# Norms by token tile, four memory slabs in the RWKV chain and two before the cross attention's queries

## The chip, the cores and the metric

One core of one Trainium2 chip runs the kernel. The metric is the device time of one execution in microseconds (us). Before the change it was 943.74 us, the median of three runs (943.54 to 943.77).

## The reference

256 tokens of width 1024 in float32 pass two blocks. Cut to what matters here:

```
h = rmsnorm(x, ln1);  z = h @ w_in            # q, k, v of three attentions, three gates
x = x + merged @ w_o
u = conv(rmsnorm(x, ln2) @ w_up);  x = x + (silu(a) * b) @ w_down
x = rmsnorm(x, ln_f)
mem_n = rms_norm(mem, mem_norm_g);  kv = mem_n @ wkv      # 1024 -> 2048
p = rms_norm(x, g[0]) @ w_in_first            # conformer conv and RWKV-7
y = concat([y_conv, y_rwkv]) @ w_out;   x = x + rms_norm(y, g[1])
q = rms_norm(x, g[2]) @ wq;  y = attention(q, kv) @ wo;   x = x + rms_norm(y, g[3])
y = swiglu(rms_norm(x, g[4]), w_gu) @ w_down; x = x + rms_norm(y, g[5])
```

rmsnorm(x, g) is x / sqrt(mean(x^2) + eps) * g along the 1024 features.

## The kernel before

**Numbers.** Every large product is made three times in fp32r: high part by high part, high by low, low by high (`three`, L1507 to L1509). An operand's high part is a ScalarE copy to fp32r (`w_hi`, `hT_hi`), its low part VectorE's difference (`w_lo`, `hT_lo`).

**Weights.** They come as 126 slabs of 1 MB in the order of their use. SyncE loads them into four buffers `raw`, ScalarE makes the high part (`split`, L457), VectorE the low part (L876), each into two buffers. TensorE waits for the low part of slab n (`lo_ready`) and signals `slab_used`, which frees the buffers for slab n+2. `splits(n)` in the programs of ScalarE and VectorE marks where in their own order slabs up to n are split.

**Products.** The tokens are two tiles (TT = 2) of 128, the features eight (KD = 8). `features` takes a slab of 256 output columns: 2 x 8 x 3 products, each with 128 columns of weights as the stationary side and all 256 tokens as the moving one. `token_products` makes results by token in the PSUM banks 4 to 7 (w_o, down, out2, wo2, down2). ScalarE and VectorE evacuate (L531 in qkv, L616 in up, L663 in in2, L804 in wq, L846 in gu2).

**A norm.** ScalarE: for each token tile a square with its sum (`sumsq`, L470) and the root (L476). VectorE: the reciprocal (L906) and x times it (`normed`, L913). When both tiles are there, TensorE transposes feature tiles 0 to 3 of both tokens into two banks and 4 to 7 after these were read (`transposes`, L1537). ScalarE copies the high part with the gain as a scale per partition (L489), VectorE makes the low part (L924). The order of all this is written out by hand in each engine's program, with semaphores between. In y1, y3 and y5 (`add_normed`) VectorE multiplies the PSUM result by reciprocal and gain row (L1420) and adds it to x (L1423).

**Memory.** The kv product of the cross attention needs only the memory tokens, so its eight slabs serve as filling: `MEM_A` = 2 after down, `MEM_B` = 5 in the RWKV chain, cut into groups of three products that `fill(point)` issues at the places listed in `MEM_FILL`, and `MEM_C` = 1 behind out2. The chain has four chunks c with the points r, u and s each, then y's sum, the products with "center" (L1996), the point gc, the head sums (L1778) and the spreads in out2's second slab.

**Queues.** GpSimd issues the small loads, the gain rows for ln_f, y1, y3 and y5 (`load_row_gain`) and the memory tokens, and multiplies the convolution's taps into diagonals (L433) after x of down is ready. ScalarE loads all masks in one DMA at the start. SyncE loads x, waits for it, loads slab 0, waits for the masks, loads the rest.

Of the kernel before, what the change touches and what calls it, by code (L numbers as in the profile page):

```python
# [17 lines left out]
F32 = mybir.dt.float32  # L18
# [31 lines left out]
MEM_A, MEM_B, MEM_C = 2, 5, 1  # L50
# [35 lines left out]
VEC_PARTS = (("ln1", 8), ("ln2", 8), ("g0", 8), ("g2", 8), ("g4", 8), ("mem_g", 8), ("mu", 14),  # L86
# [3 lines left out]
for _name, _count in VEC_PARTS:  # L90
# [6 lines left out]
TRANSPOSED = ("ln1", "ln2", "mem", "g0", "g2", "g4")  # L97
STATS = {"ln1": 0, "ln2": 1, "mem": 2, "ln_f": 3, "g0": 4, "y1": 5, "g2": 6, "y3": 7, "g4": 8, "y5": 9}
# [8 lines left out]
MASK_PARTS = (("ident", P), ("ones_head", P), ("ones_all", P), ("strict_st", CHUNK),  # L107
              ("incl_st", CHUNK), ("ident_st", CHUNK), ("scan", T), ("eps", 1), ("ln_eps", 1), ("gn_eps", 1),
# [6 lines left out]
MASK_COLS = _n  # L115
# [30 lines left out]
def mem_place(i):  # L146
# [11 lines left out]
    "consts_in", "masks_ready", "x_in", "small_in", "bias_rows_out", "bias_in", "row_gain_in", "mem_in", "y_out",  # L158
# [30 lines left out]
def transposed_bank(name, k):  # L189

    return k // 2 if name == "mem" else 2 + k // 2 % 2
# [21 lines left out]
def build(nc, x_in, mem_in, weights, fb_w, pairs_vec, vec_in, rows_in, masks_in, late_in, onehot_in, table_in,  # L213
          row_small, lora_in, bias_scratch, out):
    with ExitStack() as ctx:
# [24 lines left out]
        row_gain = sb("row_gain", [P, D])  # L240

# [41 lines left out]
        pvec = sb("pvec", [P, PAIRS, 16], F32, feed)  # L283
# [81 lines left out]
        def _(sp):  # L365
            for t in range(TT):
                sp.dma_start(x[:, t, :], x_in[0, t * P:(t + 1) * P, :]).then_inc(sems["x_in"], 16)
# [21 lines left out]
            sp.wait_ge(sems["y_out"], 16 * TT)  # L389
# [3 lines left out]
        def _(pool):  # L393
            pool.dma_start(vec[:, :], vec_in).then_inc(sems["consts_in"], 16)
# [9 lines left out]

            load_row_gain(0, 0)

# [16 lines left out]
            pool.wait_ge(sems["x_ready"], X_READY["w_o"] + TT)  # L423
# [16 lines left out]
            load_row_gain(1, 0)  # L440
            load_row_gain(2, X_READY["y1"] + TT)
            load_row_gain(3, X_READY["y3"] + TT)
# [3 lines left out]
        def _(act):  # L446
# [3 lines left out]
            act.dma_start(masks[:, 0:MASK_COLS], masks_in).then_inc(sems["masks_ready"], 16)  # L450
# [13 lines left out]
            def sumsq(name, src, waits=None):  # L464

                q = STATS[name]
                for t in range(TT):
                    if waits:
                        waits(t)
                    A(ub[:, 1, :, :, :].rearrange("p a b n -> p (a b n)") if name == "mem" else xn[:, t, :], src(t), ACT.Square,  # L470
                      accum_out=stat[:, 4 * q + t:4 * q + t + 1]).then_inc(sems["sumsq_ready"], 1)
# [11 lines left out]
            def fill_normed(name):  # L483

                z, col = TRANSPOSED.index(name), VEC["mem_g" if name == "mem" else name]
                dst = hTm_hi if name == "mem" else hT_hi
                for k in range(KD):
                    act.wait_ge(sems["xt_ready"], 4 * z + k // 2 + 1)
                    A(dst[:, k, :], ps[:, transposed_bank(name, k), k % 2 * T:k % 2 * T + T], ACT.Copy,  # L489
                      scale=vec[:, col + k:col + k + 1]).then_inc(sems["hT_hi_ready"], 1)  # L490

# [11 lines left out]
            act.wait_ge(sems["x_in"], 16 * TT)  # L503
            sumsq("ln1", lambda t: x[:, t, :])
            splits(0)
            act.wait_ge(sems["consts_in"], 16)
            fill_normed("ln1")
# [55 lines left out]
            act.wait_ge(sems["e_ready"], 1)  # L563
            A(forget[:, 1, :], forget[:, 1, :], ACT.Ln, bias=m("ones_all")[0:4, 0:1]).then_inc(sems["log1p_ready"], 1)
# [31 lines left out]
            splits(FIRST_SLAB["up"])  # L596
            sumsq("ln2", lambda t: x[:, t, :], x_tile("w_o"))
# [40 lines left out]
            fill_normed("mem")  # L638
            splits(n_a + MEM_A - 1)
# [10 lines left out]
            sumsq("ln_f", lambda t: x[:, t, :], x_tile("down"))  # L650
            sumsq("g0", lambda t: x[:, t, :], x_tile("ln_f"))
            memory_out(0)
            splits(FIRST_SLAB["in2"])
            fill_normed("g0")
            for i in range(1, MEM_A):
                memory_out(i)
# [136 lines left out]
            sumsq("y1", lambda t: banks(4 + 2 * t, 2), acc_tile("out2"))  # L793


            sumsq("g2", lambda t: x[:, t, :], x_tile("y1"))
            for i in range(8 - MEM_C, 8):
                memory_out(i)
            splits(FIRST_SLAB["wq"])
            fill_normed("g2")  # L800
            n0, u0 = FIRST_SLAB["wq"], FIRST_UNIT["wq"]
# [30 lines left out]
            splits(FIRST_SLAB["gu2"])  # L832
            sumsq("y3", lambda t: banks(4 + 2 * t, 2), acc_tile("wo2"))
# [29 lines left out]
            splits(SLABS - 1)  # L863
            sumsq("y5", lambda t: banks(4 + 2 * t, 2), acc_tile("down2"))
# [3 lines left out]
        def _(dve):  # L868
# [41 lines left out]
            def normed(name, src=None):  # L910

                for t in range(TT):
                    V.tensor_scalar(xn[:, t, :], (x if src is None else src)[:, t, :], inverse_rms(name, t), None,  # L913
                                    ALU.mult).then_inc(sems["xn_ready"], 1)

            def fill_normed(name):

                z, col = FILL[name], VEC["mem_g" if name == "mem" else name]
                low, high = (hTm_lo, hTm_hi) if name == "mem" else (hT_lo, hT_hi)
                for k in range(KD):  # L920
                    if k % 2 == 0:

                        dve.wait_ge(sems["hT_hi_ready"], KD * z + k + 2)
                    V.scalar_tensor_tensor(out=low[:, k, :], in0=ps[:, transposed_bank(name, k), k % 2 * T:k % 2 * T + T],  # L924
                                           scalar=vec[:, col + k:col + k + 1], in1=high[:, k, :].bitcast(F32),
# [6 lines left out]

            normed("ln1")
            splits(0)
            dve.wait_ge(sems["consts_in"], 16)
            dve.wait_ge(sems["masks_ready"], 16)
            fill_normed("ln1")
            splits(1)
# [215 lines left out]
            normed("mem", xn)  # L1154
            splits(n_d + 6)
            fill_normed("mem")
            splits(n_a)
            add_acc("down")
            splits(n_a + MEM_A - 1)


            dve.wait_ge(sems["row_gain_in"], 16)
            for t in range(TT):
                V.scalar_tensor_tensor(out=x[:, t, :], in0=x[:, t, :], scalar=inverse_rms("ln_f", t),
# [998 lines left out]
```

## Time and profile before

| What | us |
|---|---|
| median of the runs | 943.74 |
| profiled execution | 942.55 |
| its span | 940.3 |
| TensorE busy (x7952) | 867.8 (92%) |
| weight loads | 801.4 (85%) |
| VectorE busy | 568.4 (60%) |
| ScalarE busy | 446.1 (47%) |
| chain that ended last | PE 79%, DVE 12%, ACT 5%, issue 2%, DMA 1% |
| VectorE, one low part (L876) | 2.30 |
| ScalarE, one high part (L457) | 1.91 |
| ScalarE, square of a tile (L470) | 1.05 |
| VectorE, x times reciprocal (L913) | 0.75 |
| VectorE, L1420 and L1423, one tile each | 1.28 and 1.23 |
| VectorE, 512 columns with PSUM (L1472) | 0.69 |
| ScalarE, table load | 1.28 |

The busy shares say which engine is full. The chain shows what the end waited for. The timeline gives one engine's instructions with start and length in us; the brackets hold the idle time before an instruction and who ended it.

### The profile page before, as it was taken

To read this page: it belongs to the slowest core of one execution; us is meant where nothing else is said; L and a number is where in the kernel's file an instruction comes from. 1 tells how busy PE (TensorE), PEld (TensorE's weight loads), DVE (VectorE), ACT (ScalarE), POOL (GpSimd) and SP (SyncE) were. 2 spreads that over 40 slices of the span, in tenths; PEclk is the share of its full clock that TensorE was granted. 3 is DMA by queue.
4 is the path that set the end of the run, shared out by engine and by line. 5 is a ranking of instruction groups with operands and counts; after the bars stand their busy time and mean duration, and the time that the engine had idled before them with its cause. 6 is when DMAs were issued, how large, how long until landed. Compare 5 with 4: busy or idle time off the path is not lost.

```text
span 940.3 us, 18577 instructions
## 1 busy us (share of the span) xinstructions
PE 867.8 (92%) x7952; PEld 801.4 (85%) x7952; DVE 568.4 (60%) x686; ACT 446.1 (47%) x572; POOL 18.8 (2%) x26
## 2 busy tenths in 40 slices
PE   2999999997999999998989989997989699999996
PEld 1999989986999998887987889886967599999784
DVE  3375655475777776547589885666444555555434
ACT  4465656445655556436373402355444544444332
POOL 1100000000000000002000000000000000000000
PEclk9999999998999999999999999999999799999999
DMA  8743345444555555554533121134513355555531
GB/s 310 262 158 136 135 135 179 162 165 154 204 185 179 178 178 179 179 181 156 201 98 130 46 93 48 47 135 157 166 58 135 112 180 178 178 178 178 185 129 45
DMA packets 21100, 143.25 MB, mean 152 GB/s; under 512 B 2490, under 2 KB 2538, under 8 KB 4912
## 3 DMA queue, kind: packets, MB, share of 16 engines
q1 hardware_dynamic: 18720, 134.23, 41.5%
q0 software_dynamic: 2176, 7.27, 2.2%
q8 instruction: 50, 0.82, 0.4%
q10 hardware_dynamic: 144, 0.85, 0.2%
q14 instruction: 10, 0.08, 0.0%
HBM read 141.27 MB, written 1.07 MB: 151 GB/s over the span
## 4 chain that ended last, share of the span: by engine, by line
PE 79%; DVE 12%; ACT 5%; issue 2%; DMA 1%; SPq 0%; DVEq 0%; ACTq 0%
PE ps L1507 23%; PE ps L1509 23%; PE ps L1508 23%; DVE w_lo L876 4%; ACT w_hi L457 3%; PE ps L1859 2%; PE ps L1537 1%; PE ps L1809 1%; ACT xn L470 1%; DMA x<-in_x 1%; DVE xn L1420 1%; PE ps L2048 1%; DVE x L1423 1%; PE ps L2028 1%; DVE cacc L1189 1%
## 5 line engine op out<-in xcount | busy, mean ns | idle before, releaser
L876 DVE TENSOR_TENSOR w_lo<-raw,w_hi 128x2048 fp32r<-128x2048 f32 x126 | 289.7, 2299 | 203.6 <-ACT w_hi L457 203.6
L1507 PE MATMUL ps<-hT_hi,w_hi 128*128 128x256 f32 x1240 | 357.0, 288 | 3.7 <-DVE w_lo L876 3.7
L1508 PE MATMUL ps<-hT_lo,w_hi 128*128 128x256 f32 x1240 | 353.9, 285 | 0.0
L1509 PE MATMUL ps<-hT_hi,w_lo 128*128 128x256 f32 x1240 | 353.8, 285 | 0.0
L457 ACT ACTIVATE w_hi<-raw 128x2048 fp32r<-128x2048 f32 x126 | 240.9, 1912 | 170.7 <-PE ps L1509 169.7
L1507 PEld LDWEIGHTS ps<-hT_hi,w_hi 128*128 128x128 f32 x1240 | 240.4, 194 | 8.4 <-issue 7.2
L1508 PEld LDWEIGHTS ps<-hT_lo,w_hi 128*128 128x128 f32 x1240 | 240.1, 194 | 0.0
L1509 PEld LDWEIGHTS ps<-hT_hi,w_lo 128*128 128x128 f32 x1240 | 239.8, 193 | 0.0
L1509 PE MATMUL ps<-w_hi,gT_lo 128*128 128x512 f32 x176 | 70.0, 398 | 0.0
L1507 PE MATMUL ps<-w_hi,gT_hi 128*128 128x512 f32 x176 | 69.6, 395 | 0.1
L1508 PE MATMUL ps<-w_lo,gT_hi 128*128 128x512 f32 x176 | 69.3, 394 | 0.0
L1537 PE MATMUL ps<-masks,xn 128*128 128x128 f32 x96 | 19.4, 369 | 41.8 <-DVE xn L913 30.1
L1123 DVE SCALAR_TENSOR_TENSOR ub<-ps,pvec,ub 128x255 f32<-128x255 f32 (+1 forms) x88 | 38.4, 478 | 29.7 <-ACT ub L616 26.8
L1507 PE MATMUL ps<-w_hi,hT_hi 128*128 128x512 f32 (+2 forms) x144 | 51.6, 358 | 4.6 <-DVE w_lo L876 3.0
L1537 PEld LDWEIGHTS ps<-masks,xn 128*128 128x128 f32 x96 | 15.0, 188 | 45.5 <-DVE xn L913 16.3
L1508 PE MATMUL ps<-w_lo,hT_hi 128*128 128x512 f32 (+2 forms) x144 | 50.9, 353 | 0.0
L1509 PE MATMUL ps<-w_hi,hT_lo 128*128 128x512 f32 (+2 forms) x144 | 50.8, 353 | 0.0
L616 ACT ACTIVATE ub<-ps,pvec 128x256 f32<-128x256 f32 x44 | 22.4, 560 | 54.7 <-PE ps L1509 54.7
L1507 PEld LDWEIGHTS ps<-w_hi,gT_hi 128*128 128x128 f32 x176 | 33.0, 188 | 8.3 <-DVE w_lo L876 0.7
L1508 PEld LDWEIGHTS ps<-w_lo,gT_hi 128*128 128x128 f32 x176 | 33.0, 188 | 8.3
L1509 PEld LDWEIGHTS ps<-w_hi,gT_lo 128*128 128x128 f32 x176 | 33.0, 188 | 7.8
L1507 PEld LDWEIGHTS ps<-w_hi,hT_hi 128*128 128x128 f32 x144 | 27.2, 189 | 9.7 <-DVE w_lo L876 3.6
(277 smaller groups left out, 1040.2 us busy)
## 6 DMA issues: line engine op xcount, KB each, us to landing
raw<-in_weights SPq DMA_DIRECT2D x126, 1024.0 KB, 4.9
row_gain<-in_rows_vec POOLq DMA_DIRECT2D x4, 512.0 KB, 4.5
bias<-bias_scratch POOLq DMA_DIRECT2D x1, 1536.0 KB, 10.0
x<-in_x SPq DMA_DIRECT2D x2, 512.0 KB, 7.3
xn<-in_mem POOLq DMA_DIRECT2D x2, 512.0 KB, 4.2
out<-x SPq DMA_DIRECT2D x2, 512.0 KB, 2.6
masks<-in_masks ACTq DMA_DIRECT2D x1, 833.5 KB, 6.9
bias<-bias_scratch POOLq DMA_DIRECT2D x1, 768.0 KB, 11.6
```

The costliest lines, as they stand in the source:

```text
L457: A(w_hi[:, n % SPLIT, :], raw[:, n % RAW, :], ACT.Copy).then_inc(sems["hi_ready"], 1)
L470: A(ub[:, 1, :, :, :].rearrange("p a b n -> p (a b n)") if name == "mem" else xn[:, t, :], src(t), ACT.Square, accum_out=stat[:, 4 * q + t ...
L616: A(ub[:, p % 2, s, c, :], src[:, c * T:(c + 1) * T], ACT.Identity, bias=pvec[:, bass.ds(p + 2 * turn, 1), col + 3], scale=pvec[:, bass.ds ...
L876: V.tensor_tensor(w_lo[:, n % SPLIT, :], raw[:, n % RAW, :], w_hi[:, n % SPLIT, :].bitcast(F32), ALU.subtract).then_inc(sems["lo_ready"], 1)
L1123: ins = V.scalar_tensor_tensor(out=dst, in0=src[:, c * T:(c + 1) * T - lag], scalar=pvec[:, bass.ds(p + 2 * turn, 1), 4 * (2 * s + c) + ta ...
L1189: ins = V.scalar_tensor_tensor(out=dst, in0=src, scalar=vec[:, col:col + 1], in1=dst, op0=ALU.mult, op1=ALU.add)
L1420: do(V.scalar_tensor_tensor(out=xn[:, t, :], in0=banks(4 + 2 * t, 2), scalar=inverse_rms(name, t), in1=row_gain[:, :], op0=ALU.mult, op1=A ...
L1507: mm(dst, left[0], right[0], start=first, stop=False)
L1508: mm(dst, left[0], right[1], start=False, stop=False)
L1509: return mm(dst, left[1], right[0], start=False, stop=last)
L1537: last = nc.tensor.transpose(ps[:, transposed_bank(name, k), k % 2 * T + t * P:k % 2 * T + (t + 1) * P], xn[:, t, k * P:(k + 1) * P], ident)
L1859: last = mm(ps[to, b + q, j * CHUNK:(j + 1) * CHUNK], left[rows, 8 * q + j, :], right(rows, 8 * q + j), start=True, stop=True)
```

## The change

Norm gains ln1, ln2, g0, g2, g4 are no longer per-partition scales in the evacuation but a row, broadcast to all partitions (`norm_gain`, loaded by GpSimd before each norm) and multiplied in by VectorE together with the reciprocal. Transposes go by token tile: four features of one tile per bank. A new `features_by_token` makes the first slab of qkv, up and gu2 with 128 tokens as the moving side, first tile 0, then (in up and gu2) the transposes of tile 1, then tile 1. For g0 and g2 the transposes stand between the halves of the last memory slab, and the slab behind them is made by `features` after all operands. A dummy root (`root_table`) stands ahead of the square sums. y1, y3 and y5 multiply by the gain row first and by the reciprocal while adding. One memory slab goes from the chain to behind out2. x, masks and slabs are loaded without waits in between, the masks in two parts; the tap products on GpSimd wait for up's last low part instead of down's x.

```diff
-MEM_A, MEM_B, MEM_C = 2, 5, 1
+MEM_A, MEM_B, MEM_C = 2, 4, 2
@@ sync
             for n in range(RAW):
-                if n == 0:
-                    sp.wait_ge(sems["x_in"], 16 * TT)
-                if n == 1:
-                    sp.wait_ge(sems["masks_ready"], 16)
                 sp.dma_start(raw[:, n, :], weights[n]).then_inc(raw_in[n], 16)
...
             for t in range(TT):
-                sp.wait_ge(sems["x_ready"], X_READY["y5"] + t + 1)
-                sp.dma_start(out[0, t * P:(t + 1) * P, :], x[:, t, :]).then_inc(sems["y_out"], 16)
+                for half in range(2):
+                    cols = slice(half * 512, half * 512 + 512)
+                    sp.wait_ge(sems["x_ready"], X_READY["y5"] + 2 * t + half + 1)
+                    sp.dma_start(out[0, t * P:(t + 1) * P, cols], x[:, t, cols]).then_inc(sems["y_out"], 16)
@@ gpsimd
+            load_norm_gain("ln1")
             for src, dst in ((fb_w, fbw[:, :]), (onehot_in, onehot[:, :, :]), (table_in, table[:, :]),
...
+            pool.dma_start(vec[:, :], vec_in).then_inc(sems["consts_in"], 16)
+            pool.dma_start(masks[:, MASKS_FIRST:MASK_COLS], masks_in[:, MASKS_FIRST:MASK_COLS])\
+                .then_inc(sems["more_masks"], 16)
...
+            pool.wait_ge(sems["slab_used"], FIRST_SLAB["w_o"])
+            load_norm_gain("ln2")
             pool.wait_ge(sems["xt_ready"], 4 * (TRANSPOSED.index("ln2") + 1))
+            load_norm_gain("g0")
...
-            pool.wait_ge(sems["x_ready"], X_READY["down"] + TT)
+            pool.wait_ge(sems["g_lo_ready"], PAIRS)
@@ scalar
+            def root_table(n):
+                A(stat[:, 61 + n % 2:62 + n % 2], stat[:, 60:61], ACT.Sqrt)
+            act.wait_ge(sems["stat_set"], 1)
+            root_table(0)
+            sumsq("ln1", lambda t: x[:, t, :], lambda t: act.wait_ge(sems[f"x_in_{t}"], 16))
+            fill_normed("ln1", (0,))
             splits(0)
+            fill_normed("ln1", (1,))
             splits(1)
...
+            sumsq("ln_f", lambda t: x[:, t, :], x_tile("down"), lambda: splits(n_a + 1))
             sumsq("g0", lambda t: x[:, t, :], x_tile("ln_f"))
+            for i in range(MEM_A - 1):
+                memory_out(i)
+                splits(n_a + i + 2)
             fill_normed("g0")
+            memory_out(MEM_A - 1)
...
+            sumsq("y1", lambda t: banks(4 + 2 * t, 2), acc_tile("out2"), lambda: splits(n_c + 1))
             sumsq("g2", lambda t: x[:, t, :], x_tile("y1"))
+            for i in range(8 - MEM_C, 7):
                 memory_out(i)
+                splits(n_c + i + MEM_C - 6)
             fill_normed("g2")
+            memory_out(7)
@@ vector
+                    V.scalar_tensor_tensor(out=xn[:, t, :], in0=x[:, t, :], scalar=inverse, in1=norm_gain[:, :],
+                                           op0=ALU.mult, op1=ALU.mult).then_inc(sems["xn_ready"], 1)
...
+                        V.tensor_tensor(hT_lo[:, ks, cols], bank(transposed_half(t, half)).rearrange("p (k n) -> p k n", k=4),
+                                        hT_hi[:, ks, cols].bitcast(F32), ALU.subtract).then_inc(sems["hT_lo_ready"], 2)
...
+                    do(V.tensor_tensor(xn[:, t, :], banks(4 + 2 * t, 2), row_gain[:, :], ALU.mult))
+                    if t and between:
+                        between()
+                    inverse = inverse_rms(name, t)
+                    for part in range(parts):
+                        cols = slice(part * D // parts, (part + 1) * D // parts)
+                        V.scalar_tensor_tensor(out=x[:, t, cols], in0=xn[:, t, cols], scalar=inverse, in1=x[:, t, cols],
+                                               op0=ALU.mult, op1=ALU.add).then_inc(sems["x_ready"], 1)
@@ tensor
+            def features_by_token(n, u, name, between):
+                bank_free(u)
+                hi, lo = slab(n)
+                for t in range(TT):
+                    if t:
+                        between()
+                    cols = slice(t * P, (t + 1) * P)
+                    for c in range(2):
+                        for k in range(KD):
+                            if c == 0 and k % 4 == 0:
+                                operand(FILL[name], 4 * t + k // 2 + 1)
+                            w = slice(k * T + c * P, k * T + (c + 1) * P)
+                            last = three(ps[:, u % 2, c * T + t * P:c * T + (t + 1) * P], (hi[:, w], lo[:, w]),
+                                         (hT_hi[:, k, cols], hT_lo[:, k, cols]), k == 0, k == KD - 1)
+                return last
...
+                for i in range(first, last):
+                    for j, _ in enumerate(memory_slab(i)):
+                        if name and i == last - 1 and j == 7:
+                            transposes(name, 0)
+                            transposes(name, 1)
```

## Rows read from the trace of the kernel before

**Rows 1.** Who TensorE waited for, whole span (us in total, times, longest).
```profile
PE ps L1537 <- DVE xn L913: 30.1, 5, 15.0
...
PE ps L1537 <- DVE hT_lo L924: 11.6, 5, 3.5
```

**Rows 2.** Timeline of TensorE, two neighbouring products of 256 columns (start, length).
```profile
33.11 0.28 PE L1507 MATMUL ps<-hT_hi,w_hi 128*128 128x256 f32 x1
...
33.23 0.28 PE L1508 MATMUL ps<-hT_lo,w_hi 128*128 128x256 f32 x1
```

**Rows 3.** Timeline of TensorE, two neighbouring products of 128 columns.
```profile
73.54 0.28 PE L1507 MATMUL ps<-w_hi,hT_hi 128*128 128x128 f32 x1
...
73.65 0.28 PE L1508 MATMUL ps<-w_lo,hT_hi 128*128 128x128 f32 x1
```

**Rows 4.** Chain of work in order of time, first 20 us (start, length).
```profile
1.20 8.43 DMA x<-in_x
...
9.64 5.04 DMA raw<-in_weights
```

**Rows 5.** Timeline of the start: low part, TensorE's first product, its evacuation.
```profile
16.64 2.29 DVE L876 TENSOR_TENSOR w_lo<-raw,w_hi 128x2048 fp32r<-128x2048 f32 x1 [1.77 <-ACT w_hi L457]
...
24.32 0.58 PE L1507 MATMUL ps<-hT_hi,w_hi 128*128 128x256 f32 x1
...
31.87 0.60 ACT L531 ACTIVATE qkT<-ps 128x512 f32<-128x512 f32 x1 [6.59 <-PE ps L1509]
```

**Rows 6.** Busy time and DMA rate by stretch, 15 to 20 us (last column GB/s).
```profile
15.00:20.00 5.00, 2.16 (x9) 1.78 (x10) 3.36 (x4) 3.07 (x5) 0.00 (x0) 1.00 1.00 423
```

**Rows 7.** Timeline of norm ln2 (VectorE, ScalarE, TensorE, ScalarE).
```profile
219.93 2.44 DVE L1101 TENSOR_TENSOR x<-x,ps 128x1024 f32<-128x1024 f32 x2
...
222.34 1.28 ACT L476 ACT_TABLE_LOAD   x1
...
226.34 1.97 PE L1537 MATMUL ps<-masks,xn 128*128 128x128 f32 x8 [5.23 <-DVE xn L913]
...
237.65 1.02 ACT L616 ACTIVATE ub<-ps,pvec 128x256 f32<-128x256 f32 x2 [3.71 <-PE ps L1509]
```

**Rows 8.** Busy time by stretch in norm ln2 (PEclk is third from last).
```profile
226.00:228.00 2.00, 1.66 (x8) 1.57 (x8) 0.28 (x1) 0.51 (x2) 0.00 (x0) 0.50 0.00 0
```

**Rows 9.** Timeline of norms ln_f and g0 (GpSimd, VectorE, TensorE, ScalarE).
```profile
424.40 5.86 POOL L433 TENSOR_TENSOR stk<-masks,vec 128x992 f32<-128x992 f32 x2 [191.23 <-DVE x L1101]
...
425.03 3.44 DVE L876 TENSOR_TENSOR w_lo<-raw,w_hi 128x2048 fp32r<-128x2048 f32 x1 [0.79 <-ACT w_hi L457]
...
428.58 2.76 DVE L1164 SCALAR_TENSOR_TENSOR x<-x,stat,row_gain 128x1024 f32<-128x1024 f32 x1
...
431.44 1.29 DVE L1164 SCALAR_TENSOR_TENSOR x<-x,stat,row_gain 128x1024 f32<-128x1024 f32 x1
...
435.29 1.10 PE L1537 MATMUL ps<-masks,xn 128*128 128x128 f32 x8 [0.73 <-DVE xn L913]
...
448.45 0.84 ACT L663 ACTIVATE xn<-ps,omu 128x256 f32<-128x256 f32 x2 [3.89 <-PE ps L1509]
```

**Rows 10.** Timeline of TensorE at the end of the RWKV chain.
```profile
616.54 1.89 PE L1996 MATMUL ps<-rw,masks 128*128 128x256 f32 x8
...
621.94 0.64 PE L1778 MATMUL ps<-rw,masks 128*32 128x256 f32 x8
```

**Rows 11.** Timeline around norm g2 (first product of the memory slab, first evacuation behind).
```profile
647.87 0.28 PE L1507 MATMUL ps<-w_hi,hTm_hi 128*128 128x256 f32 x1
...
667.75 0.60 ACT L804 ACTIVATE q2T<-ps 128x512 f32<-128x512 f32 x1 [3.72 <-PE ps L1509]
```

**Rows 12.** Timeline around norm g4 (TensorE, ScalarE).
```profile
737.15 1.97 PE L1537 MATMUL ps<-masks,xn 128*128 128x128 f32 x8 [8.09 <-DVE xn L913]
...
749.00 0.60 ACT L846 ACTIVATE ub<-ps 128x512 f32<-128x512 f32 x1 [2.95 <-PE ps L1509]
```

**Rows 13.** Timeline of the end (VectorE).
```profile
936.08 1.22 DVE L1423 TENSOR_TENSOR x<-x,xn 128x1024 f32<-128x1024 f32 x1
```

More of the change, by code:

```diff
@@ L648, in memory_out @@
                 evacuated(u, A(dst, src, ACT.Copy))
[L650 removed]
+            root_table(0)
+            sumsq("ln_f", lambda t: x[:, t, :], x_tile("down"), lambda: splits(n_a + 1))
             sumsq("g0", lambda t: x[:, t, :], x_tile("ln_f"))
[L652 to L653 removed]
+            for i in range(MEM_A - 1):
+                memory_out(i)
+                splits(n_a + i + 2)
             fill_normed("g0")
[L655 to L656 removed]
+            memory_out(MEM_A - 1)
             splits(FIRST_SLAB["in2"] + 1)
@@ L1169, in _ @@
             fill_normed("g0")
+            do(V.memset(glu[:, :, 0:TAPS - 1], 0.0))
             n0, u0 = FIRST_SLAB["in2"], FIRST_UNIT["in2"]
@@ L1540, in transposes, with first_slab @@
                         last.then_inc(sems["xt_ready"], 1)
+            def features_by_token(n, u, name, between):
+                bank_free(u)
+                hi, lo = slab(n)
+                for t in range(TT):
+                    if t:
+                        between()
+                    cols = slice(t * P, (t + 1) * P)
+                    for c in range(2):
+                        for k in range(KD):
+                            if c == 0 and k % 4 == 0:
[4 more added lines that the diff above has]
+                return last
+            def first_slab(stage, name):
+                transposes(name, 0)
+                used(features_by_token(FIRST_SLAB[stage], FIRST_UNIT[stage], name, lambda: transposes(name, 1)))
             def token_products(name, left, ready):
@@ L1590, in qkv_slab @@
                     used(token_narrow(n0 + i, u0 + i, P, P))
+                elif i == 0:
+                    used(features_by_token(n0, u0, "ln1", lambda: None))
                 else:
-                    used(features(n0 + i, u0 + i, FILL["ln1"] if i == 0 else None, between=between))
+                    used(features(n0 + i, u0 + i, None, between=between))
             def forget_gates():
@@ L1718, in _, with feed_loop @@
             token_products("w_o", hT, lambda i: operand(FILL["merged"], 2 * i + 1))
-            transposes("ln2")
-            def feed_loop(name, fill):
+            def feed_loop(name, norm):
                 n0, u0 = FIRST_SLAB[name], FIRST_UNIT[name]
-                for j in range(2):
-                    used(features(n0 + j, u0 + j, fill if j == 0 else None))
+                first_slab(name, norm)
+                used(features(n0 + 1, u0 + 1, None))
                 with pe.Fori(0, (PAIRS - 1) // 2) as turn:
@@ L1760, in _, with memory_slabs @@
             operand(FILL["mem"], KD - 1)
-            for i in range(MEM_A):
-                for _ in memory_slab(i):
-                    pass
-            transposes("g0")
+            def memory_slabs(first, last, name):
+                for i in range(first, last):
+                    for j, _ in enumerate(memory_slab(i)):
+                        if name and i == last - 1 and j == 7:
+                            transposes(name, 0)
+                            transposes(name, 1)
+            memory_slabs(0, MEM_A, "g0")
             def loras():
@@ L1823, in _ @@
             for i in range(11):
-                used(features(n0 + i, u0 + i, FILL["g0"] if i == 0 else None))
+                if i == 0:
+                    operand(FILL["g0"], KD - 1)
+                used(features(n0 + i, u0 + i, None))
                 if i == 2:
@@ L2010, in _ @@
             token_products("out2", hT, out_ready)
-            for i in range(8 - MEM_C, 8):
-                for _ in memory_slab(i):
-                    pass
-            transposes("g2")
+            memory_slabs(8 - MEM_C, 8, "g2")
             n0, u0 = FIRST_SLAB["wq"], FIRST_UNIT["wq"]
+            operand(FILL["g2"], KD - 1)
             for i in range(4):
-                used(features(n0 + i, u0 + i, FILL["g2"] if i == 0 else None))
+                used(features(n0 + i, u0 + i, None))
             for u in (u0 + 2, u0 + 3):
```

157 lines of the change are left out of this document (91 added, 66 removed).

## The prediction

> **What bounds the kernel now.** I read the page's busy shares first. TensorE is busy for 92% of the span and its share of the chain that ended last is 79%, so time is won where TensorE waits, and every product added to it costs its full length. The waits of TensorE come next [rows 1]. The transposes of the norms (L1537) lead them with 30.1 and 11.6 us; no other wait on the list exceeds 6.6. The reader is to see that these stand in five places: the start, ln2, g0, g2 and g4. Then the timelines of those places, which show the engines taking turns: square sum, root, reciprocal, scaling, transposes, two evacuations, transposes, products. The windows give the clock: in ln2 it is granted at 0.50 (1.2 GHz) after TensorE stood for 5.23 us [rows 7, 8].
>
> **The price of a narrow product.** A 256-column product follows its neighbour after 0.12 us [rows 2], a 128-column one after 0.11 [rows 3]. Halving the columns saves almost nothing. `features_by_token` makes 96 narrow products where `features` made 48 wide ones: 96 x 0.111 = 10.7 us against 48 x 0.12 = 5.8. So three slabs (the first of qkv, up and gu2) cost 4.9 us more each, 14.7 in all. The first half (5.3 us) may start before the second token tile is normed, but that tile is only 1.5 us late, and after the first half its transposes (1.1), a ScalarE copy (0.6) and VectorE's difference (0.7) come in line.
>
> The Trainium skill, page TensorE: Matmul & The Clock Gate, section "Wait — 56ns, not 53.3ns?", spaces full-clock products at columns / 2.4 GHz plus 2.5 ns. By that rule a narrow one costs 56 ns and the three slabs nothing extra. The trace disagrees for this kernel's operand type: 111 ns.
>
> **Start.** Before: x is in at 9.63, the first slab lands 5.04 us later because it was issued behind x [rows 4], its low part starts at 16.64, the first product at 24.32, the first slab is through at 31.87 [rows 5]. After: the slabs are issued without waiting, and only a strip of the masks and one gain row (0.5 MB) compete. At 423 GB/s [rows 6] x, strip, gain and small loads (1.9 MB) take 4.5 us plus 2 to get going: x about 7. The rest of the masks and slab 0 (2 MB) then take 5: slab 0 at 12, bound by 9.5 (no competition) and 14.7 (as before). High part 1.9, low part 2.3: 16.2. By then both tiles are transposed (x tile 1 in at 7, square and root 1.4, VectorE 1.6, transposes to 12) and the four bias products (2.7) are out of the way. First product 16.25, 8 us sooner. The slab costs 10.7, plus about 2.4 for a low clock until about 20 to 22: done at 29.3. **-2.6** (ends: -5, and 0 if the slab comes as late as before). vec and the rest of the masks come later, with readers only behind slab 1.
>
> **ln2.** Its last product ends 5.23 us before 226.34, at 221.11. x tile 0 is ready at 221.15, its square sum at 222.3; the table load of 1.28 is gone [rows 7], since a dummy root runs while ScalarE waits. Root 222.6, reciprocal 222.8, scaling with the gain row 1.29 [rows 9] instead of 0.75: 224.2. Transposes 1.1, tile 1 is scaled until 225.65, the differences of tile 0 follow: first product 226.4. Half a slab: 231.7. Transposes 232.8, copy and difference 233.7, second half 239.1. The clock may still drop: eight transposes took 1.97 at low clock and 1.10 at full [rows 7, 9], a factor 1.8. The narrow product at low clock is shown nowhere; it lies between 0.111 and twice that, and I take 0.20 by this factor. Three us of low clock then cost 1.3; I put in 0.8. Done at 239.9 against 237.65: **+2.3** (ends +1.4, +5).
>
> **ln_f and g0.** GpSimd's tap products (5.86 us from 424.40) lie beside VectorE's low part, 3.44 instead of 2.29, and its scaling, 2.76 instead of 1.29 [rows 5, 9]: 2.6 us of the critical turn. They move to the end of the up stage, where VectorE waits over 2 us per slab; without that cover they would cost the same 2.6 there. Both memory slabs stay in front, but the transposes go between the halves of the second. Counted through: slab 1's low part moves between the two ln_f scalings and is ready at 428.5, as its slab begins; x tile 1 429.9, tile 1 scaled for g0 433.1, transposes until 434.3 with 0.5 idle, the last half until 437.1. ScalarE meanwhile splits in2's first slab and copies, VectorE's differences end at 438.9: 1.9 us idle instead of 0.73 and 3.3. The wide slab ends at 444.8 against 448.45 [rows 9]: **-3.6** (ends -5, -2). The memset of glu moves behind the fill, 0.16.
>
> **RWKV chain.** Sixteen memory groups (one slab, 5.8 us) leave it. The groups come in order, so the last sixteen go: two in u3, four in s3, ten in gc. The first saves 0.7 and y follows 0.7 sooner. Four groups covered y's sum (1.2 us on VectorE), which now stands open: the center products at 616.54 [rows 10] come 1.0 sooner. Ten groups (3.6 us) lay between these and the head sums at 621.94 [rows 10]; only ScalarE's two squares (1.1) are needed there: 3.3 sooner in all. out2's second slab has its high part early, and the head spread keeps its distance. **-3.3** (ends: -5.8 all of it, 0 if the chain hides nothing).
>
> **y1 and g2.** That slab comes back here. The products of out2 end at 647.9 [rows 11]. ScalarE splits the second memory slab (1.9) before it squares tile 1, so its sum is at 650.9 instead of 649. VectorE multiplies by the gain row ahead of the root, then the low part, then adds: tile 0 649.6, low part 654.45 (TensorE waits 0.7 for it), x tile 1 655.95, g2 scaled 657.45 and 659.1. Transposes 657.5 to 660.25, last half of the slab 663.1. High part, four copies, low part, four differences: 665.0. The wide slab ends at 670.85 against 667.75: **+3.1** (ends +1, +5). So the slab's move alone is worth about nothing.
>
> **y3 and g4.** The products end 8.09 before 737.15, at 729.06 [rows 12]. Without the table load and with the product ahead of the root, x tile 0 is ready 1.7 us sooner, tile 1 at 732.95, tile 0 scaled for g4 734.45. TensorE has stood for 5.4 us and I expect a low clock: transposes 736.5, first product 736.95, low clock until about 739.6, first half 743.5, transposes, copy and difference 745.5, second half 750.9 against 749.0: **+1.9** (ends +0.4, +4.5).
>
> **y5.** Tile 1 is now bound by its square sum at 933.1: product 1.2, root and reciprocal beside it, two halves of 0.65: 935.9 against 937.3 [rows 13]. The last DMA is half as large, 0.3 less by estimate (512 KB landed after 2.6). **-1.7** (ends -1.2, -2.5).
>
> The loads of the other gain rows and of pvec are issued on GpSimd well before their readers (g0's ahead of the memory tokens, which have 130 us) and cost nothing; if one were late its norm would wait up to 4.5 us for it. g4's row waits for g2's scaling and has some 70 us.
>
> **Sum.** -2.6 + 2.3 - 3.6 - 3.3 + 3.1 + 1.9 - 1.7 = -3.9. The profiled execution took 942.55 (span 940.3 and 2.25 around it): 938.6. It was 1.19 faster than the median of the runs, 943.74; against that the change gives **939.8 us**.
>
> **Rivals.**
> 1. Good start and full clock: slab 0 lands at 10 to 11 and TensorE is already at full clock behind its transposes (-5), ln2 at +1.4, g4 at +0.4, the rest as above: -8.7, 935.0. For it: x needs no more than its own 1 MB at 423 GB/s. Against it: the clock was low in every wait of over 5 us.
> 2. Even: the unblocked slabs slow x and the gain row, so the start gives 0, the rest stands: -1.3, 942.4. The Trainium skill, page DMA: Bandwidth & Descriptors, section "Issuing engines are not separate DMA queues", says that DMAs of all issuers interleave on the same 16 engines. By that rule the gain row on GpSimd's queue is served beside the slabs; no row of this trace shows such a pair.
> 3. Slower: the low clock stays through the narrow first half. 48 x 0.20 = 9.6 instead of 5.3 us in the start, in ln2 and in g4: against my sum (which has 2.4, 0.8 and 1.3 of it) +8.4, so +4.5 and 948.2. It decides for slower once the three slabs together lose over 5.8 us more than I have. For it: rows 8 and the half-clock transposes of g4 [rows 12]. Against it: the products run without a pause once begun.
> 4. The narrow product needs 56 ns. The three slabs then cost 5.4 each: -3.9 - 15.8, 924.0. Rows 3 speak against it.
> 5. The dummy root does not do what it says, a later function reloads the table: 1.28 back in ln2, g4 and y5: -0.1, 943.7. For it speaks nothing in the code: no other function stands between the dummy and the square sum.
>
> **How the numbers follow.** Forecast 0.50, rival 1 0.18, rival 2 0.13, rival 3 0.14, rival 4 0.02, rival 5 0.03. From no change this kernel's measurement tells about 0.2%, 1.9 us. Faster: the forecast's part (0.45 of 0.50), rivals 1 and 4, 0.02 of rival 2: 0.67. Slower: rival 3 and a little of 2: 0.14 to 0.15. Same: 0.18. The range reaches into rivals 1 and 3: 934.5 to 944.5; the forecast's own is 937 to 942.5.
>
> **What would show it.** First evacuation of the qkv stage (L531 before) at 29.3; first ones of up at 2.3 later, of in2 3.6 sooner, of wq 3.1 later and of gu2 1.9 later than before, each after subtracting the shift of what lies in front. Products of 128 columns 0.111 apart. Head sums 3.3 us sooner after the start of in2. No table load between a square sum and its root except for the memory. It is wrong if the narrow products are spaced otherwise, if slab 0 lands before 10 or after 14, or if the chain keeps its length without its sixteen groups.

## The result and the profile after

The kernel became slower: 971.48 us, the median of four runs (969.95 to 972.59), beside 943.75 for the kernel before, measured alongside (four runs), a ratio of 1.029, with [1.027, 1.031] as its 95% interval. The forecast was 939.8. The profiled execution took 969.95, its span is 968.2.

The page of the changed kernel: busy time of TensorE and of its weight loads, and the granted clock in 40 slices.

```profile
PE 906.9 (94%) x8096; PEld 843.6 (87%) x8096; DVE 567.7 (59%) x669; ACT 440.3 (45%) x557; POOL 21.3 (2%) x32
...
PEclk8699999998699999999999999999999589999999
```

TensorE gained 39.1 us of busy time, with 144 more products. The slices show three dips of the clock, and they are the three slabs made by token: slices 1 and 2, 10 and 11, 32 and 33.

The first reading of a stage is ScalarE's first evacuation of its PSUM results, the moment at which the first slab is through. The five that answer to [rows 5, 7, 9, 11, 12]: start, length, operation, idle time before.

```profile
39.18 0.60 ACT L559 ACTIVATE qkT<-ps 128x512 f32<-128x512 f32 x1 [19.55 <-PE ps L1566]
...
258.40 1.02 ACT L646 ACTIVATE ub<-ps,pvec 128x256 f32<-128x256 f32 x2 [8.74 <-PE ps L1566]
...
465.97 0.84 ACT L694 ACTIVATE xn<-ps,omu 128x256 f32<-128x256 f32 x2 [5.20 <-PE ps L1566]
...
684.55 0.60 ACT L836 ACTIVATE q2T<-ps 128x512 f32<-128x512 f32 x1 [5.17 <-PE ps L1566]
...
777.85 0.60 ACT L879 ACTIVATE ub<-ps 128x512 f32<-128x512 f32 x1 [7.44 <-PE ps L1566]
```

Against before they come 7.3, 20.7, 17.5, 16.8 and 28.8 us later. Taking off what lies in front of each norm gives its own part:

| Part | forecast | measured |
|---|---|---|
| start | -2.6 | +7.3 |
| ln2 | +2.3 | +12.4 |
| ln_f and g0 | -3.6 | -3.8 |
| RWKV chain | -3.3 | -3.5 |
| y1 and g2 | +3.1 | +2.8 |
| y3 and g4 | +1.9 | +12.0 |
| y5 | -1.7 | -2.0 |
| the stretches behind the three slabs, low clock in their first products | 0 | +2.7 |
| sum | -3.9 | +27.9 |

Each row is the change between two marks, taken from the one profiled execution of either kernel. Four terms are within 0.3, and one of these, the chain, does not hold in other executions (see e4). The error lies in the three parts with narrow products and in the slabs behind them. The +2.7 is a net: 13, 9 and 22 wide products at 0.213 instead of 0.12 us are +4.1 of it by estimate, and the rest of these stretches is that much shorter than before. The timeline of TensorE at the start shows them from first to last, and the wide ones behind:

```profile
18.40 0.48 PE L1564 MATMUL ps<-hT_hi,w_hi 128*128 128x128 f32 x1 [2.12 <-DVE w_lo L910]
18.67 0.41 PE L1565 MATMUL ps<-hT_lo,w_hi 128*128 128x128 f32 x1
18.88 0.41 PE L1566 MATMUL ps<-hT_hi,w_lo 128*128 128x128 f32 x1
...
38.72 0.41 PE L1566 MATMUL ps<-hT_hi,w_lo 128*128 128x128 f32 x1
38.94 0.52 PE L1564 MATMUL ps<-hT_hi,w_hi 128*128 128x256 f32 x1
...
41.60 0.34 PE L1564 MATMUL ps<-hT_hi,w_hi 128*128 128x256 f32 x1
41.79 0.28 PE L1565 MATMUL ps<-hT_lo,w_hi 128*128 128x256 f32 x1
```

The 96 narrow products (128 columns on the moving side; wide ones have 256) run 0.213 us apart from 18.4 to 38.9, 20.5 us, with no pause. The wide ones behind are 0.213 apart too, until 41.6; then they fall to 0.12. The windows say that this is the clock (length; busy time of PE, PEld, DVE, ACT, POOL; granted clock; DMA share; GB/s):

```profile
17.00:39.00 22.00, 20.60 (x97) 20.61 (x97) 4.92 (x6) 2.62 (x4) 3.11 (x4) 0.52 0.75 264
39.00:42.00 3.00, 3.00 (x16) 3.00 (x16) 0.39 (x1) 2.40 (x2) 0.00 (x0) 0.55 0.00 0
42.00:60.00 18.00, 18.00 (x155) 16.68 (x154) 9.76 (x9) 8.52 (x9) 0.00 (x0) 1.00 0.47 157
...
235.00:258.00 23.00, 22.31 (x104) 21.91 (x104) 4.35 (x4) 2.99 (x3) 2.11 (x4) 0.50 0.34 130
258.00:261.00 3.00, 3.00 (x18) 3.00 (x18) 1.44 (x4) 2.60 (x3) 0.00 (x0) 0.64 0.02 5
261.00:280.00 19.00, 19.00 (x159) 18.91 (x158) 13.65 (x19) 11.57 (x14) 0.00 (x0) 1.00 0.44 150
```

The granted clock is 0.50 (1.2 GHz) as long as these rows of narrow products run, though TensorE is busy throughout, and returns to 1.00 (2.4 GHz) 2 to 5 us after wide ones begin (2.0 in ln2, 2.7 in the start, 4.7 in g4, which is not shown). In ln2 both halves show it, each 10.3 us long where the forecast had 5.3; these rows answer to [rows 7]:

```profile
232.52 1.67 PE L1592 MATMUL ps<-masks,xn 128*128 128x128 f32 x8 [3.11 <-DVE xn L949]
...
234.97 0.45 PE L1564 MATMUL ps<-hT_hi,w_hi 128*128 128x128 f32 x1 [0.78 <-DVE hT_lo L958]
...
245.24 1.93 PE L1592 MATMUL ps<-masks,xn 128*128 128x128 f32 x8
...
247.86 0.48 PE L1564 MATMUL ps<-hT_hi,w_hi 128*128 128x128 f32 x1 [0.69 <-DVE hT_lo L958]
```

The waits did what the change is for. TensorE's longest, which answers to [rows 1]:

```profile
PE ps L1592 <- DVE xn L949: 21.3, 5, 11.6
```

The transposes waited 41.7 us before and wait 21.3 now. The time shown as busy is the price.

### The profile page after: what moved, and what is told of

It is laid out like the page before. It is cut to its first block, busy times and chain, and to the rows that moved or that the text cites. A ratio compares the mean times of both kernels' runs of the same rounds, so it can differ in the third digit from the quotient of the medians.

```text
span 968.2 us, 18891 instructions
## 1 busy us (share of the span) xinstructions
PE 906.9 (94%) x8096; PEld 843.6 (87%) x8096; DVE 567.7 (59%) x669; ACT 440.3 (45%) x557; POOL 21.3 (2%) x32
## 4 chain that ended last, share of the span: by engine, by line
PE 80%; DVE 12%; ACT 5%; issue 3%; DMA 1%; DVEq 0%; ACTq 0%; POOLq 0%
PE ps L1564 24%; PE ps L1566 23%; PE ps L1565 23%; DVE w_lo L910 4%; ACT w_hi L468 3%; PE ps L1956 2%; PE ps L1904 1%; DMA norm_gain<-in_rows_vec 1%; DVE xn L949 1%; PE ps L2143 1%; PE ps L2123 1%; PE ps L1592 1%; DVE xn L1473 1%; DVE cacc L1241 1%; DVE hT_lo L958 1%
## 5 line engine op out<-in xcount | busy, mean ns | idle before, releaser
L1564 PE MATMUL ps<-hT_hi,w_hi 128*128 128x256 f32 (+1 forms) x1288 | 382.6, 297 | 11.9 <-DVE w_lo L910 5.8
L1565 PE MATMUL ps<-hT_lo,w_hi 128*128 128x256 f32 (+1 forms) x1288 | 379.6, 295 | 0.0
L1566 PE MATMUL ps<-hT_hi,w_lo 128*128 128x256 f32 (+1 forms) x1288 | 379.4, 295 | 0.0
L1564 PEld LDWEIGHTS ps<-hT_hi,w_hi 128*128 128x128 f32 x1288 | 263.3, 204 | 18.0 <-issue 10.1
L1565 PEld LDWEIGHTS ps<-hT_lo,w_hi 128*128 128x128 f32 x1288 | 263.4, 205 | 0.0
L1566 PEld LDWEIGHTS ps<-hT_hi,w_lo 128*128 128x128 f32 x1288 | 263.3, 204 | 0.0
L1592 PE MATMUL ps<-masks,xn 128*128 128x128 f32 x80 | 15.1, 354 | 21.3 <-DVE xn L949 21.3
L1162 DVE TENSOR_TENSOR gT_lo<-ub,gT_hi 128x512 f32 (+1 forms) x22 | 15.2, 689 | 29.8 <-ACT gT_hi L887 29.1
```

The lines of the kernel that those rows point to most:

```text
L1162: V.tensor_tensor(gT_lo[:, bass.ds(2 * p + 4 * turn, 2), :], ub[:, p % 2, 1, :, :], gT_hi[:, bass.ds(2 * p + 4 * turn, 2), :].bitcast(F32) ...
L1564: mm(dst, left[0], right[0], start=first, stop=False)
L1565: mm(dst, left[0], right[1], start=False, stop=False)
L1566: return mm(dst, left[1], right[0], start=False, stop=last)
L1592: last = nc.tensor.transpose(ps[:, transposed_half(t, half), k * P:(k + 1) * P], xn[:, t, (4 * half + k) * P:(4 * half + k + 1) * P], ident)
```

## Experiments

Theory A: a row of 96 narrow products does not lift the low clock with which it begins, so each slab made by token takes some 20 us. A1 and A2 say what such a row does to a full clock that it is given: in A1 it keeps it, in A2 it loses it. B: the clock is low only because of the wait ahead of the transposes; narrow products would be cheap if they began at full clock.

### e1_wide_all: the three first slabs made by wide products

```diff
-                used(features_by_token(FIRST_SLAB[stage], FIRST_UNIT[stage], name, lambda: transposes(name, 1)))
+                transposes(name, 1)
+                used(features_when_both(FIRST_SLAB[stage], FIRST_UNIT[stage], name))
...
-                    used(features_by_token(n0, u0, "ln1", lambda: None))
+                    used(features_when_both(n0, u0, "ln1"))
```

`features_when_both` makes the same slab by 48 products of 256 columns once both tiles are transposed.

> The changed kernel with the first slabs of qkv, up and gu2 made by wide products (256 tokens) once both tiles are transposed. Theory A (128-column products cannot bring TensorE back to full clock, 256-column ones do): the clock rises inside each of the three slabs, each done 10 to 13 us sooner than in the changed kernel, 931 to 934 us in all. Theory B (the pause and the transposes in front keep the clock low, whatever the products' width): the wide slabs also run to their end at half clock, 48 x 0.213 = 10.2 us instead of 20.5, about 940 us.

928.63 us, a ratio of 0.984 [0.982, 0.985] to before, some 2 us better than expected by A: the sign turned, with everything else of the change left in. TensorE and ScalarE in ln2 and g4:

```profile
219.49 3.32 PE L1592 MATMUL ps<-masks,xn 128*128 128x128 f32 x16 [3.11 <-DVE xn L949]
...
223.94 0.36 PE L1564 MATMUL ps<-hT_hi,w_hi 128*128 128x256 f32 x1 [1.13 <-DVE hT_lo L958]
...
229.96 1.02 ACT L646 ACTIVATE ub<-ps,pvec 128x256 f32<-128x256 f32 x2 [4.65 <-PE ps L1566]
...
724.31 3.49 PE L1592 MATMUL ps<-masks,xn 128*128 128x128 f32 x16 [5.81 <-DVE xn L949]
...
728.77 0.36 PE L1564 MATMUL ps<-hT_hi,w_hi 128*128 128x256 f32 x1 [0.97 <-DVE hT_lo L958]
...
734.80 0.60 ACT L879 ACTIVATE ub<-ps 128x512 f32<-128x512 f32 x1 [3.20 <-PE ps L1566]
```

The slab waits for both tiles, which costs 1.7 to 2.0 us more from the first transpose to the first product, and then takes 6.0 instead of 23.4. The wait of 5.81 ahead of g4's transposes is as long as in the changed kernel, and the clock fell there too: the wait alone is not what made 777.85 out of 749.00. But in this execution ln2 and g4 don't show wide products lifting the clock. It was back before the first of them, at the end of the sixteen transposes (of 128 columns each, so what theory A says is shown for the slab's products and not for every narrow product). In g4 it was back at 727.5, ahead of the first wide product at 728.77. The windows of ln2:

```profile
220.00:222.30 2.30, 2.30 (x12) 2.26 (x11) 1.78 (x3) 1.19 (x2) 0.00 (x0) 0.50 0.01 4
222.30:229.00 6.70, 5.57 (x47) 5.36 (x46) 4.22 (x4) 2.90 (x3) 2.11 (x4) 1.00 0.63 218
```

Wide products that begin at low clock are in e1's start, where they ran 0.213 apart from 18.91 to 24.17 and then 0.12, and in ln2 and g4 of e5 below. Each time the clock came back within the slab, after 4.5 to 5.3 us. That wide products are followed by the full clock where narrow ones are not rests on these places and on the slabs behind the narrow ones in the changed kernel, and theory B's forecast of a slab at half clock to its end falls with them.

### e2_warm_gu2 and e3_narrow_g0: narrow products that begin at full clock

```diff
                 transposes(name, 0)          # e2, ahead of it, for gu2 alone:
+                    for _ in range(13):
+                        mm(bank(u % 2), ident, masks[:, P:P + 512], start=True, stop=True)
...
-                used(features(n0 + i, u0 + i, None))          # e3, in2's first slab
+                    used(features_by_token(n0, u0, "g0", lambda: None))
```

> The changed kernel with 13 added 512-column products of constants (results unused) on TensorE in its pause before the transposes of g4, so that the clock is full when the narrow products of gu2's first slab begin. If narrow products hold the clock and only fail to raise it (theory A1), both halves take 5.3 us, transposes 1.1 each: the slab is done about 11 us sooner, 959 to 960. If narrow products also lose it (A2), the clock falls inside the first half and the gain is 2 to 5 us, 965 to 968.

> The changed kernel with in2's first slab also made by 96 narrow products, at a place where the clock is full and stays so. A1 (held): +4.9 us, 975. A2 (lost after a while): the clock falls within the 10.7 us of narrow products, +7 to +14 us, 977 to 984.

e2 took 967.10 in its one run, inside A2's range, but in another way than expected. A constant product of 512 columns took some 0.87 us there, so the thirteen ran 5.3 us into the time of the transposes. They kept the clock full, and it was lost only in the second narrow half (windows as above, then single products):

```profile
759.10:764.80 5.70, 5.63 (x51) 5.66 (x52) 0.52 (x1) 0.00 (x0) 0.00 (x0) 1.00 0.00 0
766.70:769.00 2.30, 2.28 (x20) 2.29 (x21) 1.37 (x2) 2.28 (x2) 0.00 (x0) 0.98 0.03 7
769.00:775.30 6.30, 6.30 (x31) 6.30 (x31) 1.48 (x1) 0.46 (x1) 0.00 (x0) 0.50 0.48 166
```

```profile
768.78 0.30 PE L1564 MATMUL ps<-hT_hi,w_hi 128*128 128x128 f32 x1
768.89 0.41 PE L1565 MATMUL ps<-hT_lo,w_hi 128*128 128x128 f32 x1
769.10 0.42 PE L1566 MATMUL ps<-hT_hi,w_lo 128*128 128x128 f32 x1
```

The first half takes 5.4 us at 1.00. In the second the spacing goes from 0.11 (768.78 to 768.89) to 0.21 (768.89 to 769.10) in the middle of a row without a wait. e3 asks the same where a wide slab stands in front: 990.42 in its one run, above the 977 to 984 of A2, and the clock falls 2.6 us after the first narrow product.

```profile
461.70:464.30 2.60, 2.58 (x23) 2.60 (x24) 1.77 (x2) 0.85 (x1) 0.00 (x0) 0.98 0.71 293
464.30:480.20 15.90, 15.90 (x76) 15.90 (x76) 0.58 (x1) 0.00 (x0) 0.00 (x0) 0.50 0.19 66
```

in2's first reading moved from 465.97 to 480.20, +14.2. The 4.7 us beyond lie in the RWKV chain (201.1 us instead of 194.3, a length that varies by 4.6 between executions, see e4), the wide products of its first slab among them, at low clock until 484.6. B falls and A2 holds in both runs: full clock at the start of the row does not last through 96 products.

How long it lasts is not one figure. It was 2.6 us in e3 and 9.7 in e2 (2.0 of them transposes and waits), and the kernel before has a row of 48 narrow products (slab 6 of qkv, from which [rows 3] is taken) that keeps it for its whole 5.3 us. Its first and last product, 47 steps of 0.111 apart:

```profile
72.92 0.22 PE L1507 MATMUL ps<-w_hi,hT_hi 128*128 128x128 f32 x1
...
78.12 0.28 PE L1509 MATMUL ps<-w_hi,hT_lo 128*128 128x128 f32 x1
```

### e8_before_narrow: the narrow slabs alone, in the kernel before

```diff
-                    used(features(n0 + j, u0 + j, fill if j == 0 else None))
+                    used(features_narrow(n0, u0, fill) if j == 0 else features(n0 + j, u0 + j, None))
...
-                    used(features(n0 + i, u0 + i, FILL["ln1"] if i == 0 else None, between=between))
+                elif i == 0:
+                    used(features_narrow(n0, u0, FILL["ln1"]))
```

> The kernel before with only its first slabs of qkv, up and gu2 made by 96 narrow products each, all else as before. If the narrow products keep the clock low until the next wide ones (theory A), each of the three takes 20.5 us plus about 1 in the slab behind: 983 to 989 us. If a narrow product cost only its 0.111 us and the changed kernel's loss lay in its new order, 956 to 960.

989.42 in its one run, at the upper end of what theory A gave, span 987.2: 46.9 over before. Taken the other way round, from the changed kernel (968.2) to e1 (923.0), the narrow slabs are worth 45.2 us. So the change is a loss of some 46 in three slabs and a gain of some 18 in everything else, and the parts nearly add. That the width of the products in the three slabs makes the loss is shown from both kernels. The window of its g4:

```profile
766.00:796.00 30.00, 25.91 (x120) 25.38 (x121) 8.05 (x14) 9.45 (x15) 0.69 (x1) 0.50 0.15 53
```

### e4_wide_chain5: e1 with the memory slab back in the chain

```diff
-MEM_A, MEM_B, MEM_C = 2, 4, 2
+MEM_A, MEM_B, MEM_C = 2, 5, 1
```

> e1_wide_all with five memory slabs in the RWKV chain and one behind out2, as before. If the sixteen last groups cost the chain 3.5 us and the slab behind out2 is covered by the norm's turns, this is 3 to 5 us slower than e1_wide_all. If moving the slab is worth nothing, as the sum of the prediction said (-3.3 and +3.1), within 1 us of it.

929.26 against 928.63, both at a ratio of 0.983 to 0.984 with the interval [0.982, 0.985]. From in2's first reading to the end of y1's first square it took 198.5 us instead of 196.4, from there to wq's first reading 23.4 instead of 24.3. The slab's place is worth nothing that can be measured in the whole kernel.

The same stretch of the chain shows how far a single execution can be trusted. Its code is the same in the changed kernel and in e1, e2, e5, e6 and e7, yet it took 194.3, 196.4, 194.4, 198.3, 197.1 and 198.9 us, against 197.8 before. In e1 the centre products to the head sums took 4.57 us where the changed kernel took 3.26, at a granted clock of 0.50 from 604.8 to 608.

### e5_gain_act: e1 with the first gain row on ScalarE's queue

```diff
-            load_norm_gain("ln1")
...
+            act.dma_start(norm_gain[:, :], rows_in[4].partition_broadcast(P)).then_inc(sems["first_gain_in"], 16)
```

> e1_wide_all with ln1's gain row loaded from ScalarE's queue, right behind the strip of masks, instead of from GpSimd's. If the late gain row (VectorE waited 3.7 us for it, until 10.2) is what made the start late, the scaling begins at 6 to 7, the first product 2 us sooner (16.5 instead of 18.9) and the kernel is 1.5 to 2.5 us faster than e1_wide_all. If the first slab's split binds anyway, no difference.

927.72, ratio 0.983 [0.980, 0.985], not to be told from e1; the expected 1.5 to 2.5 us did not come. ScalarE and VectorE at its start:

```profile
7.93 1.06 ACT L485 ACTIVATE xn<-x 128x1024 f32<-128x1024 f32 x1 [1.75 <-DMA x<-in_x]
...
9.05 1.28 DVE L949 SCALAR_TENSOR_TENSOR xn<-x,stat,norm_gain 128x1024 f32<-128x1024 f32 x1 [2.68 <-DMA norm_gain<-in_rows_vec]
```

The row is there about 1 us sooner, not 3 to 4, and x's second tile, squared at 6.12 in the changed kernel, comes 1.8 later, as if the loads shared what there is. The first reading of qkv comes at 26.20 instead of e1's 27.32.

### e6_warm and e7_all: wide products in the pauses

```diff
+                for _ in range({"up": 3, "gu2": 6}[stage]):
+                    mm(bank(u % 2), ident, masks[:, P:P + 512], start=True, stop=True)
                 transposes(name, 0)
                 transposes(name, 1)
```

e6 is e1 with this; the added products give nothing to the result. e7 is e6 with e5's queue, eight added products of 256 columns ahead of the first transposes and two behind the bias products.

> e1_wide_all with 3 and 6 added 512-column products of constants (results unused) in TensorE's pauses before the transposes of ln2 and g4. If the low clock behind these pauses (3.4 and 6.8 us in e1_wide_all) is what still costs there, each sixteen transposes take 2.2 instead of 3.4 us: 1.5 to 3 us faster than e1_wide_all. If the clock falls anyway, no difference or up to 1 us slower.

> e5_gain_act and e6_warm together, and added products of 256 columns of constants (results unused) at the very start (8) and behind the bias products (2), so that the first slab begins at full clock. If each part gives what is expected, 5 to 7 us faster than e1_wide_all, 921 to 924. If the clock at the start rises no sooner, 3 to 5 us.

e6: 923.20 (922.58 to 923.95), ratio 0.978 [0.976, 0.980]; e7: 922.98 (921.05 to 923.29), ratio 0.977 [0.975, 0.979]. Both are 5 to 6 us faster than e1: e7 as expected, e6 by more than its 1.5 to 3. e7 has the lowest median here and is not to be told from e6. Its first reading of qkv came at 24.38 against e6's 26.71, but the clock returned at 19.1, three us into the first slab and not before it, and its chain was 1.8 us longer. TensorE of e6 in ln2 (eight transposes per tile, the first tile's are shown), then its windows of ln2 and g4:

```profile
216.42 1.88 PE L1641 MATMUL ps<-masks 128*128 128x512 f32 x4
218.84 1.09 PE L1592 MATMUL ps<-masks,xn 128*128 128x128 f32 x8 [0.54 <-DVE xn L949]
```

```profile
217.00:221.00 4.00, 2.95 (x17) 1.65 (x16) 3.42 (x6) 2.68 (x6) 0.00 (x0) 1.00 0.48 203
...
720.00:727.00 7.00, 5.54 (x24) 2.85 (x22) 6.54 (x10) 4.57 (x10) 0.53 (x1) 1.00 0.40 156
```

The clock no longer falls in ln2 and g4: eight transposes take 1.09 where e1's sixteen took 3.32. Against e1's profiled execution that is only 0.8 us of span; but that execution was e1's fastest (924.77, the others up to 929.94), and e6's all lie within 1.4. What the others of e1 lose can be read from e5, whose products are e1's and whose profiled execution took 929.79. Its windows of ln2 and g4:

```profile
223.00:229.00 6.00, 6.00 (x34) 6.00 (x35) 2.76 (x2) 1.47 (x1) 1.38 (x3) 0.61 0.85 304
...
726.00:736.00 10.00, 8.00 (x36) 7.56 (x37) 7.68 (x8) 6.73 (x9) 0.53 (x1) 0.50 0.16 52
```

Here the clock came back only within the wide slab. From the last square to the first reading it took 13.4 us in ln2 and 13.0 in g4, in e1's profile 11.2 and 10.9: 4.3 us by the moment at which the clock returns. In e6, where it never goes, the two took 10.6 and 10.4, 5.4 less than in e5 together. That is as much as e6 gains on e1 in the median (5.4), if e1's other executions are like e5's; their traces are not there to show it.

## Why the prediction was wrong

**The price of a narrow product: the step that failed.** The forecast took 0.111 us for nearly all of the 96 and let the low clock end by itself: at 20 to 22 in the start, within three us in ln2, at 739.6 in g4. In its place the runs showed 0.213 for all 96 in each of three slabs. By its own terms: the start's slab took 20.8 instead of 13.05 (+7.7), ln2's two halves 20.6 instead of 10.6 and 0.8 for the clock, with slower transposes between them (+10.1 in all), g4 the same (+10.1); +2.7 net in the stretches behind, from low clock. That is 30.6 of the 31.8 us between -3.9 and +27.9.

**Where the reading went astray.** The 0.111 came from a place where narrow products follow wide ones at full clock [rows 3]. They are a row of 48, 5.3 us, at full clock from its first product to its last. It tells what a product costs at that clock; it says nothing about a row that begins at the low one, as all three did, and nothing sure about one twice as long. The sentence "Against it: the products run without a pause once begun" took it that a row without pauses brings the full clock. Rival 3 had the right mechanism and broke off too soon: it kept the low clock for the first half only and so reached 948.2. Had it said that nothing in the slab lifts the clock, its sum would have been 3 x 96 x 0.20 = 57.6 us for the slabs instead of the 32.1 + 4.5 of the forecast: 21 more, 961, on the side on which the result lies.

**What the profile before could have said.** In g4 the transposes stood at 1.97 and the wide slab behind them was through 9.9 us after their end [rows 12]: low clock at first, full soon after. In between lie the other transposes and wide products. No row showed a recovery within narrow products, and the upper bound for each of the three slabs should have been low clock to its end. The range ended at 944.5 because that end was missing.

**Start.** x was squared at 4.68, sooner than the 7 expected, but the gain row came late. The longest stretch of the chain at the start, and VectorE's first scaling:

```profile
1.25 8.81 DMA norm_gain<-in_rows_vec
```

```profile
10.16 1.29 DVE L949 SCALAR_TENSOR_TENSOR xn<-x,stat,norm_gain 128x1024 f32<-128x1024 f32 x1 [3.74 <-DMA norm_gain<-in_rows_vec]
```

From there the chain runs through tile 0's transposes and copy (until 14.2) to the high part of slab 0 (14.12), which stands behind that copy in ScalarE's program though the slab had landed at 11.1 (issued at 1.7, 9.4 us to landing), 12 by the forecast. First product 18.40, not 16.25: +2.15 of the start's error, rival 2's mechanism in part. By the Trainium skill, page DMA: Bandwidth & Descriptors, section "Issuing engines are not separate DMA queues", a row on another queue shares the engines with the slabs; the trace agrees (8.8 us for 512 KB, where the five such rows have a median of 4.3), and e5, where moving the row gained 1 us and cost x's second tile 1.8, fits. With wide products the start is a gain: first reading 27.32 in e1, against 31.87.

**ln_f and g0, y5: right.** -3.8 for -3.6 and -2.0 for -1.7. VectorE's scaling takes 1.28 both times, the tap products no longer stand beside it. The last two halves of y5, which answer to [rows 13], take 1.42 from 964.29.

**g2: right; the RWKV chain: right in this execution, not shown beyond it.** g2 is +2.8 for +3.1, and the part is 24.3 us long in every execution with two memory slabs there. The chain is -3.5 for -3.3; the head sums at 635.93 stand against 621.94 in [rows 10] when all has moved by 17.5, which is 3.5 sooner. But with the same chain e1 is at -1.4, e6 at -0.7, e5 at +0.4 and e7 at +1.1 (e4's section), so the close match is in part luck. That the slab's move is worth nothing held in e4.

**Rivals 1, 4 and 5.** Full clock in the three slabs did not come, so rival 1 is out. The narrow product at full clock is 0.11 (48 of them in e2's 5.4 us), so 56 ns is out. The Trainium skill, page TensorE: Matmul & The Clock Gate, section "LDWEIGHTS (loading the stationary operand)", gives a weight load of 128 columns 107 ns by its formula; the trace is nearer to that than to 56. No table load stood between a square sum and its root, so rival 5 is out.

**What stays open.** Both widths are 0.213 apart at low clock, and the weight loads are busy 21.91 of 22.31 us in the narrow stretch, so the weight load probably sets the pace; no run took it away. Why these rows of 96 are granted only the low clock is not told by any run: they show that it is so. Nor is it told why full clock lasted 2.6 us in e3, 9.7 in e2 and through all 48 products in the kernel before. Every profiled execution, those of both kernels included, has one to three further low stretches between g0 and g2, of 3 to 8 us; what brings them, and whether the groups missing from the chain do, is open too. e2, e3 and e8 stand on one run each.

## What to carry to other kernels

Splitting a product by tokens to start it sooner halves the work of each instruction but not its time, and a long row of such products can run at half clock from end to end; take the price of a new shape from a row of its own length that begins as yours will, or bound it by the low clock throughout. When a busy engine's time grows without new waits, look at the granted clock of that stretch before anything else. Here waiting for both tiles and making the three slabs by wide products turned +2.9% into -1.6%, and throw-away wide products in two pauses made it -2.2% (e6).

## What the runs showed of the hardware that was not expected

- 96 products of 128 columns, back to back for 20.5 us, left the clock at 0.50. The Trainium skill, page TensorE: Matmul & The Clock Gate, section "Why this matters for your kernels", advises to keep TensorE busy without a break to reach full throughput; here TensorE was busy 20.60 of 22.00 us and did not reach it, and the measurement decides.
- Such rows lost a full clock 2.6 us (e3) and 9.7 us (e2, with 2.0 us of transposes and waits between) after they began, while a row of 48 in the kernel before kept it for 5.3 us.
- Sixteen transposes of 128 columns, 3.3 to 3.5 us, ended with the clock back at 1.00 in e1's ln2 and g4, before any wide product; in e5 the same sixteen did not (0.50 from 219.0 to 223.2).
- At low clock products of 128 and 256 columns cost the same 0.213; at full clock 0.111 and 0.12.
- The record of the clock can be wrong at the start of a span. In e8 it says 1.00 while the products run at the low pace. The window and two products of that run:

```profile
23.00:45.00 22.00, 22.00 (x100) 20.72 (x99) 3.00 (x5) 2.28 (x4) 3.11 (x4) 1.00 0.56 184
```

```profile
24.59 0.41 PE L1508 MATMUL ps<-hT_lo,w_hi 128*128 128x128 f32 x1
24.81 0.41 PE L1509 MATMUL ps<-hT_hi,w_lo 128*128 128x128 f32 x1
```

The pace, 0.213, is the surer sign there; this run's record shows its first change only in ln2. In the changed kernel it reads 1.00 until about 17.9, though sixteen transposes took 3.31 us from 11.59 on, as long as e1's in ln2 at 0.50 (3.32).
